# Residuals of a split-float weight stream on one engine, and another order of the recurrent branch's first stage

## What is computed

```python
def first_block(x, ...):
    xn = rmsnorm(h, norm_mix_g)                       # x * rsqrt(mean(x^2) + eps) * g
    q, k, v, xr, gr, ga, gb = split(xn @ w_in)        # w_in: 1024 x 7168
    ya = chunked_band_attention(q, k, v, rel_table) @ w_attn_out
    xc = sum(xr_padded[:, j:j+S] * conv_w[j] for j in range(4)) + conv_b
    r, i = sigmoid(xc @ w_r + b_r), sigmoid(xc @ w_i + b_i)    # 16 diagonal blocks of 64
    a = exp(-8 * r * softplus(-lam))
    hr = scan(a, sqrt(1 - a^2) * i * xc)              # h[t] = a[t] h[t-1] + bx[t]
    yb = (hr * gelu(gr)) @ w_rnn_out
    h = h + (sigmoid(ga + ..) * ya + sigmoid(gb + ..) * yb) @ w_o
    # then rmsnorm and a gated feed-forward block
```

## Time and profile before

| | us |
|---|---|
| median of 3 runs (984.08 to 986.66) | 986.62 |
| the profiled execution | 987.3 |
| its span, first to last instruction | 985.5 |
| TensorE busy | 953.0 |
| VectorE busy | 508.4 |
| ScalarE busy | 486.6 |
| GpSimd busy | 341.9 |

### The profile page before, as it was taken

One profiled execution on the slowest core, in us unless ns is written; L12 is line 12 of the kernel. 1 busy time (PEld: TensorE's weight loads), 2 busy tenths in 40 slices (PEclk: granted clock), 3 DMA queues, 4 the chain that ended last, 5 costly groups with the idle time before them and its releaser, 6 DMA issues.

```text
span 985.5 us, 14443 instructions
## 1 busy us (share of the span) xinstructions
PE 953.0 (97%) x4870; PEld 805.4 (82%) x4870; DVE 508.4 (52%) x840; ACT 486.6 (49%) x763; POOL 341.9 (35%) x170
## 2 busy tenths in 40 slices
PE   8989999999999999999999999999999989999997
PEld 7979988888788888888878888877878768888886
DVE  4956965454643443432654434347488774334332
ACT  5347545654354445434644444437436564454442
POOL 1622001003444434434433444643412033443442
PEclk9999999999999999999999999999999999999999
DMA  6645573444546656779465655545502256655552
GB/s 224 193 166 152 177 234 119 144 149 169 186 145 186 190 174 190 257 225 245 150 192 180 189 185 190 189 151 175 181 28 86 86 157 197 193 178 184 187 186 82
DMA packets 132770, 169.32 MB, mean 172 GB/s; under 512 B 16707, under 2 KB 88430, under 8 KB 132598
## 3 DMA queue, kind: packets, MB, share of 16 engines
q1 hardware_dynamic: 132566, 168.67, 54.6%
q10 hardware_dynamic: 160, 0.07, 0.0%
HBM read 167.61 MB, written 1.10 MB: 171 GB/s over the span
## 4 chain that ended last, share of the span: by engine, by line
PE 84%; DVE 9%; ACT 3%; issue 2%; DMA 1%; POOL 0%; DVEq 0%; POOLq 0%; SPq 0%; ACTq 0%
PE acc L783 23%; PE acc L785 23%; PE acc L784 23%; PE tp L856 4%; DVE w_lo L1183 2%; PE acc L838 2%; PE acc L842 2%; PE acc L840 2%; DVE u L1283 1%; PE sc L926 1%; ACT w_hi L469 1%; PE acc L1118 1%; ACT junk L475 1%; DVE u L1280 1%; DVE xt_lo L1588 1%
## 5 line engine op out<-in xcount | busy, mean ns | idle before, releaser
L469 ACT ACTIVATE w_hi<-w_raw 128x1024 fp32r<-128x1024 f32 x305 | 322.2, 1060 | 374.9 <-PE acc L785 325.9
L1802 POOL TENSOR_TENSOR w_lo<-w_raw,w_hi 128x1024 fp32r<-128x1024 f32 x124 | 307.1, 2478 | 410.8 <-ACT w_hi L469 410.7
L1183 DVE TENSOR_TENSOR w_lo<-w_raw,w_hi 128x1024 fp32r<-128x1024 f32 x181 | 235.4, 1305 | 308.0 <-ACT w_hi L469 306.9
L783 PE MATMUL acc<-w_hi,xt_hi 128*128 128x512 f32 (+1 forms) x752 | 298.6, 397 | 5.7 <-DVE w_lo L1183 2.8
L785 PE MATMUL acc<-w_lo,xt_hi 128*128 128x512 f32 (+1 forms) x752 | 292.9, 390 | 0.0
L784 PE MATMUL acc<-w_hi,xt_lo 128*128 128x512 f32 (+1 forms) x752 | 292.4, 389 | 0.0
L783 PEld LDWEIGHTS acc<-w_hi,xt_hi 128*128 128x128 f32 x752 | 141.3, 188 | 35.8 <-DVE w_lo L1183 3.6
L785 PEld LDWEIGHTS acc<-w_lo,xt_hi 128*128 128x128 f32 x752 | 141.1, 188 | 29.5
L784 PEld LDWEIGHTS acc<-w_hi,xt_lo 128*128 128x128 f32 x752 | 141.4, 188 | 27.4
L783 PE MATMUL acc<-w_hi,hid_hi 128*128 128x512 f32 x264 | 103.2, 391 | 0.0
L785 PE MATMUL acc<-w_lo,hid_hi 128*128 128x512 f32 x264 | 102.8, 389 | 0.0
(11 more groups left out here) (209 smaller groups left out, 902.4 us busy)
## 6 DMA issues: line engine op xcount, KB each, us to landing
w_raw<-in_ffn_w_gu SPq DMA_DIRECT2D x176, 256.0 KB
w_raw<-in_w_in SPq DMA_DIRECT2D x68, 512.0 KB
w_raw<-in_w_ffn_in SPq DMA_DIRECT2D x88, 256.0 KB
w_raw<-in_ffn_w_down SPq DMA_DIRECT2D x44, 512.0 KB
w_raw<-in_w_ffn_out SPq DMA_DIRECT2D x22, 512.0 KB
w_raw<-in_w_rnn_out SPq DMA_DIRECT2D x8, 512.0 KB
w_raw<-in_w_attn_out SPq DMA_DIRECT2D x8, 512.0 KB
w_raw<-in_w_o SPq DMA_DIRECT2D x8, 512.0 KB
```

What stands on the lines that cost most here:

```text
L469: act.activation(w_hi[:, b, :], w_raw[:, b, :], ACT.Copy).then_inc(hi_done[b], 1)
L783: pe.matmul(o, hi[:, k, rows], wh, start=first and n == 0, stop=False)
L1183: dve.tensor_tensor(w_lo[:, b, :], w_raw[:, b, :], w_hi[:, b, :].bitcast(F32), ALU.subtract).then_inc(lo_done[b], 1)
L1802: pool.tensor_tensor(w_lo[:, b, :], w_raw[:, b, :], w_hi[:, b, :].bitcast(F32), ALU.subtract).then_inc(lo_done[b], 1)
```

## The change

`lo_on_dve` gives VectorE every slab below 80. Of 0 to 79, GpSimd had the odd ones from 5 to 19 and from 61 to 79.

In the first stage: the parameters are turned ahead of rstd and both ahead of slab 4; the inputs of softplus, its Exp and four of its steps go ahead of the spreading of rstd, its other steps behind the residual of slab 14; the first tap of the convolution, with its bias, is taken by ScalarE (`first_taps`, a new semaphore `conv_first`), the other three stay with VectorE; the gates' products come one tile after each of slabs 9 to 16 instead of two after each of 12 to 15; their tanhs follow ScalarE's copies of slabs 13 to 20 one by one, the two GELU calls come behind the fourth and the seventh tile, and `consts_ready` is waited for behind the last. In the merge, the residuals of 75 to 79 and ScalarE's copies of 76 to 79 change their places in the queues.

```diff
-X = starts([("x", 4), ("rs", 1), ("par", 1), ("gate", 8), ("p1", 16), ("at", 4), ("mt", 4), ("h1", 4),
+X = starts([("x", 4), ("par", 1), ("rs", 1), ("gate", 8), ("p1", 16), ("at", 4), ("mt", 4), ("h1", 4),
...
-        return q % 2 == 0 or q < 4 or 20 <= q < 60 or S["in2"] <= q < S["in2"] + 4 or S["out2"] + 4 <= q < S["f3i"] + 4
+        return q % 2 == 0 or q < S["f1i"] or S["in2"] <= q < S["in2"] + 4 or S["out2"] + 4 <= q < S["f3i"] + 4
...
-            feed(4, 6)
             act.wait_ge(abs_lam, 1)
             act.activation(small[:, 1, :], small[:, 0, :], ACT.Exp, scale=-1.0).then_inc(exp_lam, 1)
-            feed(10, 6)
-
-            def gelu(g):
-
-                for b in range(2):
-                    wait_drained(act, g, b)
-                    v = grT[:, 4 * (g - 2) + 2 * b:4 * (g - 2) + 2 * b + 2, :]
-                    act.activation(v, v, ACT.Gelu_apprx_tanh).then_inc(gelu_done, 1)
-
-            gelu(2)
-            act.wait_ge(consts_ready, 1)
-            for n in range(KT):
-                if n % 2 == 0:
-                    feed(16 + n // 2, 1)
+
+            def first_taps(g):
+
+                wait_both_drained(act, g)
+                for n in range(4 * g, 4 * g + 4):
+                    act.activation(xcT[:, n, :], xrT[:, n, 0:T], ACT.Identity,
+                                   scale=par[:, PAR["conv_w"] + n:PAR["conv_w"] + n + 1],
+                                   bias=par[:, PAR["conv_b"] + n:PAR["conv_b"] + n + 1]).then_inc(conv_first, 1)
+
+            def gate_tanhs(n):
                 x = X["gate"] + n
                 wait_tp_full(act, x)
                 act.activation(trT[:, n, :], tp[x % 2][:, 0:T], ACT.Tanh, scale=0.5,
                                bias=small[:, 8, n:n + 1]).then_inc(gates_done, 1)
                 act.activation(ti[:, n, :], tp[x % 2][:, T:2 * T], ACT.Tanh, scale=0.5,
                                bias=small[:, 9, n:n + 1]).then_inc(tp_free[x % 2], 1)
...
+            feed(4, 4)
+            act.wait_ge(set_up, 2)
+            first_taps(0)
+            feed(8, 4)
+            first_taps(1)
+            feed(12, 1)
+            for n in range(4):
+                feed(13 + n, 1)
+                gate_tanhs(n)
+            gelu(2)
+            for n in range(4, 7):
+                feed(13 + n, 1)
+                gate_tanhs(n)
             gelu(3)
-
+            feed(20, 1)
+            gate_tanhs(7)
+
+            act.wait_ge(consts_ready, 1)
             act.wait_ge(conv_done, KT)
             for n in range(KT):
-                if n % 2 == 0:
+                if n % 2 == 0 and n > 0:
                     feed(20 + n // 2, 1)
...
-            feed(S["attn"] + 11, 2)
+            feed(S["attn"] + 11, 1)
             for n in range(2, 4):
                 split(X["mt"] + n, None, None, yt_hi[:, 2 * n:2 * n + 2, :], 0.5)
-            feed(S["o"] + 5, 3)
...
-            def turn_rs_and_parameters():
-
+            def turn_parameters():
+
+                pe.wait_ge(par_landed, 16 * 15)
+                turn(X["par"], [(0, par_rows[0:PAR["end"], :])])
+
+            def turn_rs():
                 pe.wait_ge(rs_spread, 1)
                 turn(X["rs"], [(m * P, rs_cols[:, m, :]) for m in range(MT)])
-                pe.wait_ge(par_landed, 16 * 15)
-                turn(X["par"], [(0, par_rows[0:PAR["end"], :])])
-
-            def gates(n0):
+
+            def gates(n):
                 pe.wait_ge(bd_landed, 64)
-                for n in (n0, n0 + 1):
-                    x = X["gate"] + n
-                    pe.wait_ge(conv_done, n + 1)
-                    wait(pe, tp_free[x % 2], x // 2)
-                    pe.matmul(tp[x % 2][:, 0:T], blockdiag[:, n, :], xcT[:, n, :], start=True, stop=True)
-                    pe.matmul(tp[x % 2][:, T:2 * T], blockdiag[:, KT + n, :], xcT[:, n, :], start=True,
-                              stop=True).then_inc(tp_full[x % 2], 1)
-
-            group_turned(0, 0, ready=pairs_ready(X["x"]), after={0: lambda: turn_x(2), 1: lambda: turn_x(3)})
-            group_turned(4, 1, after={0: turn_rs_and_parameters})
-            group_turned(8, 2)
-            group_turned(12, 3, after={q: lambda q=q: gates(2 * q) for q in range(4)})
-            for g in range(4, 8):
+                x = X["gate"] + n
+                pe.wait_ge(conv_done, n + 1)
+                wait(pe, tp_free[x % 2], x // 2)
+                pe.matmul(tp[x % 2][:, 0:T], blockdiag[:, n, :], xcT[:, n, :], start=True, stop=True)
+                pe.matmul(tp[x % 2][:, T:2 * T], blockdiag[:, KT + n, :], xcT[:, n, :], start=True,
+                          stop=True).then_inc(tp_full[x % 2], 1)
+
+            def gates_after(slabs):
+                return {q: lambda n=n: gates(n) for q, n in slabs.items()}
+
+            group_turned(0, 0, ready=pairs_ready(X["x"]),
+                         after={0: lambda: turn_x(2), 1: lambda: turn_x(3), 2: turn_parameters, 3: turn_rs})
+            group_turned(4, 1)
+            group_turned(8, 2, after=gates_after({1: 0, 2: 1, 3: 2}))
+            group_turned(12, 3, after=gates_after({0: 3, 1: 4, 2: 5, 3: 6}))
+            group_turned(16, 4, after=gates_after({0: 7}))
+            for g in range(5, 8):
...
-            mean_square("x")
...
+            wait_tp_full(dve, X["par"])
+            dve.tensor_copy(par[:, 0:PAR["end"]], tp[X["par"] % 2][:, 0:PAR["end"]]).then_inc(tp_free[X["par"] % 2], 1)
+            wait_tp_free(dve, X["par"])
+            dve.tensor_scalar(small[:, 8, :], pcol("b_r"), 0.5, None, ALU.mult)
+            dve.tensor_scalar(small[:, 9, :], pcol("b_i"), 0.5, None, ALU.mult)
+            dve.tensor_tensor(small[:, 11, :], pcol("fin_g"), pcol("f2_g"), ALU.mult)
+
+            dve.tensor_scalar(small[:, 10, :], pcol("lam"), -1.0, 0.0, ALU.mult, ALU.max)
+            step(dve.scalar_tensor_tensor(small[:, 0, :], pcol("lam"), -1.0, pcol("lam"), ALU.mult, ALU.max))
+            dve.memset(free_marks[:, 5:6], 0.0).then_inc(abs_lam, 1)
+            mean_square("x")
+            dve.wait_ge(exp_lam, 1)
+            step(dve.tensor_scalar(small[:, 2, :], small[:, 1, :], 2.0, None, ALU.add))
+            step(dve.reciprocal(small[:, 3, :], small[:, 2, :]))
+            step(dve.tensor_tensor(small[:, 2, :], small[:, 1, :], small[:, 3, :], ALU.mult))
+            step(dve.tensor_tensor(small[:, 4, :], small[:, 2, :], small[:, 2, :], ALU.mult))
             dve.wait_ge(rs_done, NTH["x"])
             rx = rs[:, ST["x"]]
             dve.tensor_copy(rs_cols, rx.unsqueeze(2).to_broadcast([P, MT, P])).then_inc(rs_spread, 1)
-            feed(4, 4)
+            feed(4, 2)
             wait_tp_full(dve, X["rs"])
             step(dve.tensor_copy(rx_row[:, 0, :], tp[X["rs"] % 2][:, 0:T]))
-            dve.tensor_scalar(rx_row[:, 1, :], tp[X["rs"] % 2][:, 0:T], HD ** -0.5, None,
-                              ALU.mult).then_inc(tp_free[X["rs"] % 2], 1)
-            wait_tp_full(dve, X["par"])
-            dve.tensor_copy(par[:, 0:PAR["end"]], tp[X["par"] % 2][:, 0:PAR["end"]]).then_inc(tp_free[X["par"] % 2], 1)
...
-            wait_tp_free(dve, X["rs"])
             evict_turned(0, to_xr)
-            wait_tp_free(dve, X["par"])
-
-            step(dve.scalar_tensor_tensor(small[:, 0, :], pcol("lam"), -1.0, pcol("lam"), ALU.mult, ALU.max))
...
+            dve.tensor_scalar(rx_row[:, 1, :], tp[X["rs"] % 2][:, 0:T], HD ** -0.5, None,
+                              ALU.mult).then_inc(tp_free[X["rs"] % 2], 1)
+
...
                 base_step = steps[0]
-                for j in range(4):
+                dve.wait_ge(conv_first, tiles[-1] + 1)
+                for j in range(1, 4):
                     for at, n in enumerate(tiles):
-                        tap = xrT[:, n, j:j + T]
-                        w = par[:, PAR["conv_w"] + 8 * j + n:PAR["conv_w"] + 8 * j + n + 1]
-                        if j == 0:
-                            ins = dve.tensor_scalar(xcT[:, n, :], tap, w, pcol("conv_b", 1, n), ALU.mult, ALU.add)
...
-                            ins = dve.scalar_tensor_tensor(xcT[:, n, :], tap, w, xcT[:, n, :], ALU.mult, ALU.add)
+                        if j > 1:
+                            dve.wait_ge(dve_step, base_step + (j - 2) * len(tiles) + at + 1)
+                        ins = dve.scalar_tensor_tensor(xcT[:, n, :], xrT[:, n, j:j + T],
+                                                       par[:, PAR["conv_w"] + 8 * j + n:PAR["conv_w"] + 8 * j + n + 1],
+                                                       xcT[:, n, :], ALU.mult, ALU.add)
...
+            feed(6, 1)
             wait_both_drained(dve, 0)
             conv_tiles((0, 1))
-            feed(8, 2)
+            feed(7, 2)
             conv_tiles((2, 3))
             evict_turned(1, to_xr)
-            feed(10, 2)
+            feed(9, 2)
             wait_both_drained(dve, 1)
             conv_tiles((4, 5))
-            feed(12, 2)
+            feed(11, 1)
             conv_tiles((6, 7))
-            dve.wait_ge(exp_lam, 1)
```

(30 more changed lines are left out.)

6 lines of the change are left out of this document (removed).

## The result

| | before | after |
|---|---|---|
| median, us | 986.31 (4 runs, 984.08 to 986.66) | **974.06** (4 runs, 973.97 to 974.38) |
| ratio, 95% interval | | 0.9876 (0.9864 to 0.9888) |
| the profiled execution, us | 987.3 | 973.97 |
| its span, us | 985.5 | 972.1 |

What follows compares the result with a forecast made beforehand. TensorE, busy 97% of the span, was taken as the bound, its waits decided by VectorE's queue. First stage 8.8 plus merge 3.8, less 0.3, gave 12.3 us and a forecast of 974.4 us, eight in ten within 971.8 to 979.

Steps and rivals of the forecast that it cites:

- First stage, 8.8 us: First stage: 6.36 us idle, 0.2 of other waits, 0.5 for modelled ends and 1.7 low clock won.
- The walk through VectorE's queue: First stage: VectorE ends residual 9 at 38.3 against 39.0, the tightest place, and residual 10 at 39.5 against 42.7.
- Slab 4's start, +0.2: Before slab 4: softplus steps moved ahead of the spreading of rstd delay its start 0.2 us, bounds 0 to +0.8.
- -10.4 against +6.8, so the move is needed: First stage, VectorE: six moved residuals add 6.8 us; the 10.4 us by which GpSimd's residuals stretched its instructions go.
- Gates and tanhs: First stage, ScalarE: tanhs no longer wait for `consts_ready`; the 4.23 us idle before the second pair of gates goes.
- The merge, 3.8 us: Merge: without GpSimd's residual of slab 75 between VectorE's adds, 2.1 us idle and 1.7 of slow matmuls are won.
- The margin of 0.3: Taken off the total gain of 12.6 us for margins of 0.1 to 0.7 us at slab 9 and the merge.
- Half of stage one: Rival: VectorE reaches residual 9 or 10 late by 1 to 3 us, slab 10's stall moves: 975.5 to 978; 0.10.
- Slower: Rival, first stage: a residual costs VectorE 2.99 us whenever DMA and ScalarE are busy: 993 us; chance 0.03.
- The stretch isn't GpSimd's doing: Rival, first stage: the 10.4 us of excess on VectorE stay: 985 us, no change to speak of; chance 0.05.
- Loads can't keep up: Rival, first stage: below 240 GB/s slabs 12 to 19 come late; 978.8 us at 210 GB/s; chance 0.04.
- The merge stall stays: Rival, merge: VectorE has more residuals ahead of the adds and comes later than 264.9: 978.2 us; chance 0.08.

Runs made afterwards that it cites:

- both cuts undone: Changed kernel with the old assignment of residuals (odd slabs 5 to 19 and 61 to 79 on GpSimd) and first taps back on VectorE: 979.29 us.
- assignment alone: Kernel before with only the new `lo_on_dve` (all residuals below slab 80 on VectorE), every order old: 980.55 us, ratio 0.9953.
- gates alone: Kernel before with only ScalarE's order changed: gate tanhs ahead of both GELU passes, no longer waiting for `consts_ready`: 981.38 us.
- two runs with idle work: Changed kernel plus unneeded work on GpSimd in the first stage: subtractions that read and write, 984.04 us; memsets that only write, 976.15 us.
- idle subtractions: Changed kernel with six unneeded 128x1024 subtractions on GpSimd beside the residuals of slabs 5 to 15: 984.04 us, ratio 0.9977.

## Why the prediction was right, and where its steps were not

The number was right, 0.3 us off, and so was the mechanism of each stall. Step by step:

*What bounds the kernel.* TensorE, with VectorE's queue late in the first stage: held. The run with both cuts undone has TensorE waiting for residuals again at two places.

*First stage, 8.8 us.* Measured 9.3 between checkpoints. Idle time 6.36 and low clock 1.7 are as read from the rows. Of the 0.5 above the sum 0.3 is no gain: the turns of rstd and the parameters stand behind slab 4's start before (slab 5 starts at 27.52, 3.21 us later instead of 2.88) and ahead of it after. The other 0.2 stays unexplained.

*The walk through VectorE's queue.* With slab 4 at 22.75 instead of 24.5, everything is 1.75 us earlier: residual 9's end, forecast at 38.3, would be 36.55, and the first of the two at 35.17 ends about 36.3; slab 9, forecast for 39.0, begins at 37.24. The margin was 0.9 where 0.7 was forecast. The first taps on ScalarE take

```profile
36.59 2.06 ACT L509 ACTIVATE u<-xrT,par 128x256 f32<-128x256 f32 x4
38.56 1.04 ACT L469 ACTIVATE w_hi<-w_raw 128x1024 fp32r<-128x1024 f32 x1
```

1.97 us for four by spacing, 2.0 in the sum. VectorE waited for them once, 0.25 us (37.77 above). The loads moved 228 GB/s without TensorE waiting for any; 240 were forecast.

*Slab 4's start, +0.2.* Within 0 to 0.3: six profiled executions in the new order with the clock up at the start have slab 4 at 22.75 to 23.02, the two in the old order at 22.75 and 22.93. In the two executions of the result x's landing and the clock moved it by more than that. The wait there fell from 0.35 to 0.19 us, as the moved turn of rstd should make it.

*Residuals: "-10.4 against +6.8, so the move is needed".* This step failed. The excess is real and it did go, but in the new order TensorE doesn't need it gone: with 5 to 19 on GpSimd the time is 974.18 and the first stage as long to 0.01 us. Nor did the other parts take the excess away. In that run it is 9.4 us: 1.75 and 2.15 on the taps at 27.52 and 32.79, 1.0 on residual 10 (38.52), 2.1 on the later taps, 2.2 on the first softplus step, 0.2 on residual 6. It falls on whatever VectorE has there. I had set 10.4 us against 6.8 over the whole stretch; what counts is what stands ahead of a deadline, and the one that was missed before is slab 10's. Residual 10 ended 19.9 us behind slab 4's start before (44.23 - 24.31). In the new orders either cut alone brings it inside the 18.05 that it has. Undoing both costs 3.8 us more, so VectorE's load does decide, but as one margin that several cuts share.

*Gates and tanhs.* Held: the 4.23 us were ScalarE's order, and the move of two lines in the kernel before takes them away. The table load between the tanhs (at 53.39, 1.28 us) stayed covered. Slab 16 begins at 63.20; with the start 1.75 later that would be 64.95, and 65.5 to 66.5 was forecast.

*The merge, 3.8 us.* The checkpoints give 3.74, the three runs with 61 to 79 on GpSimd in the new order only 2.1 more than the changed kernel, and 1.6 and 1.2 by the medians. The idle part (1.9 to 2.1) is shown. The 1.7 us of low clock stood behind this stall in the three profiled executions with the old order (before, assignment alone, gates alone: 0.72, 0.72 and 0.67 in the 5 to 6 us behind it) and in none of the three with the new order in which the same 1.9 us stall was left (256.41, 256.38, 260.99: 1.00). Why is open: one execution each is too few to tell a rule from chance, and the stalls of the two groups look alike in the trace. So 3.7 us is what the whole change brought here, and 2.1 of it what the forecast gave as the cause.

*The margin of 0.3.* No wait behind slab 4 or at the merge took it. The total still matched, and with differences between executions of 1 to 2 us (the start, the clock near 780) an error of 0.3 us in 12 is partly luck.

That the sum still came out has one reason of its own: the terms were of stalls, not of parts. Each stall was priced once, and all were taken away; how much each part of the change contributed had no place in the sum, and there I was wrong. The low clock was counted behind two of the three stalls, as the one trace had it; other executions have it otherwise (it follows slab 10's stall in the gates alone, and not the gates' shorter one in the assignment alone).

*Rivals.* "Half of stage one" fell: no wait behind slab 4, and 0.9 us in hand at slab 9. "Slower" fell at the first residual: 1.21 to 1.23 us each, with DMA at 228 GB/s and ScalarE awake. "The stretch isn't GpSimd's doing" fell by the two runs with idle work. "Loads can't keep up" by the stretch with no wait. "The merge stall stays" came true only for the assignment without the order.

## What to carry to other kernels

Price stalls, then undo the parts one by one *and two by two*: two cuts that each cost nearly nothing when undone were worth 3.8 us together here, because they share one margin. Time them at a place of the trace that both kernels have, too, since medians also hold what the start and the clock do elsewhere. Before moving element-wise work to GpSimd, look for VectorE instructions that end together with GpSimd's: what they lose (2.2 us for an instruction of 0.2 to 1.2) can exceed what is unloaded, and it matters where such an instruction stands just ahead of a wait of TensorE. A wait in an in-order queue costs what is queued behind it: ask first whether it can stand later.

## What the runs showed of the hardware

The same stall isn't always followed by the low clock. Behind the wait of 2.35 us near 780 to 795 us TensorE's matmuls stood 0.43 us apart in the changed kernel's profiled execution, and 0.23 as usual in a second one of the same kernel. Of the fourteen profiled executions three have the low clock there: this one, the one with 5 to 19 on GpSimd (granted clock 0.58 from 781.9 to 786 us) and the idle subtractions (0.57 from 789 to 793). So one profile can hold 1 to 2 us that the next one doesn't.

GpSimd's write-only memset doesn't touch a VectorE instruction with two SBUF inputs (2.34 us for two residuals) but stretches a copy of 0.29 us to 2.65. A short instruction pays as much as a long one: the eight elements of a softplus step took 2.36 us instead of 0.17 beside a residual on GpSimd (with 5 to 19 there, at 51.04), and the residual 38.52 in the same run 2.23 instead of 1.21.
